# Two thirds of the modulation product moved from TensorE to GpSimd and from the first stages of layer 0 into its attention

## The chip, the cores and the metric

The kernel runs on one core of one Trainium2 chip. The metric is the device time of one execution in microseconds (us). Three runs of the kernel before gave 3046.41, 3048.2 and 3042.95 us: a median of 3046.41 us. TensorE's granted clock has two levels, 1.2 and 2.4 GHz; the profile writes it as a share of the upper one.

## What is computed

A sequence of 1024 tokens with 1024 channels goes through two layers of one block (a gated convolution beside an attention that picks 256 keys for each query), then through one layer of a second block (two recurrences and a feed-forward part). The change touches only how the first block is modulated:

```python
c_act = jax.nn.silu(c)                                   # (1, 1024)
for l in range(2):
    mod = c_act @ w_ada[l] + b_ada[l]                    # (1, 3072)
    shift, scale, gate = jnp.split(mod, 3, axis=-1)
    h = rmsnorm(x, g_pre[l]) * (1.0 + scale[:, None, :]) + shift[:, None, :]
    ...                                                  # h @ w_in, convolution, key search, attention
    x = x + gate[:, None, :] * rmsnorm(y, g_post[l])
```

`c_act @ w_ada[l]` is a product of one row with a 1024 x 3072 matrix in float32. Layer 0 needs its shift and scale before its first projection, its gate only when its output is added to x; layer 1's shift and scale are needed at the end of layer 0, its gate later still.

## The kernel before

**The product in pieces.** `w_ada` comes in 48 pieces of 256 rows by 512 columns (512 KB each, two blocks of 128 rows side by side in SBUF). The list `ADA_PIECES` (line 472) orders them: pieces 0 to 15 are shift and scale of layer 0 (four column blocks n = 0 to 3 of four pieces), 16 to 23 the gate of layer 0 (n = 4, 5), 24 to 31 the gate of layer 1, 32 to 47 shift and scale of layer 1. `ada_piece` (lines 677 to 682) makes two float32 products with 512 columns for each piece. The stationary operand `cb[l]` is `c_act` repeated over 128 columns, so that every partition of the PSUM result holds the same row. Eight products, from four pieces, add up one column block.

**Where the pieces stand on TensorE.** Pieces 0 to 15 run first (line 866). Each other piece is put between other work of layer 0 by `ada_pieces` (line 686): one behind each of the eight groups of transposes of x (`transpose_x`, pieces 16 to 23), eight between the blocks of the index scores (line 934, pieces 24 to 31), and sixteen inside the first two convolution projections (`conv_in` of `wg0` and `wv0`, line 806, pieces 32 to 47).

**What VectorE does with the results.** `gate_sum` (line 1910) adds a gate row of 1024 from PSUM to the bias, `gate_gain` (line 1916) multiplies it by `g_post`. `columns` (line 1889) turns a block of 512 shift or scale values from a row into a column per channel, with a multiplication by the identity and a reduction. `gains` (line 1903) adds the bias and `g_pre`. Those of layer 1 and both gates run beside the search for the key threshold (`beside`, line 2172), which is VectorE's main work after the index scores. `ht_part` (line 1964) scales and shifts the transposed x of layer 0: for each of eight groups one `TENSOR_SCALAR` from PSUM (L1972) and two subtractions (L1980); ScalarE does three operations for the same group (L1330, L1333, L1335).

**Queues.** SyncE issues the weight loads in the order in which they stand in its program (lines 503 to 565). A piece's buffer is one of four (`ADA`, then `ADA2`); piece i waits until piece i - 4 has been multiplied. The other weights come in chunks of 1 MB through two raw buffers (`stage`); GpSimd splits each chunk into a high and a low bf16 part (`CAST` at L646, `TENSOR_TENSOR` at L653; 4 of each for one chunk) into a ring of four. It may overwrite a slot only when TensorE has used the chunk four before it. Pieces 28 to 47 stand in SyncE's program behind chunk `cv1` and ahead of `wv1`.

**Attention of layer 0.** From about 486 to 680 us a loop over 64 steps i = 8 tb + h (query block tb, head h) runs on TensorE, VectorE and ScalarE (lines 1035 to 1053 and 2318 to 2363). In step i TensorE makes the logits of step i, the weighted sums of steps i - 3 and i - 5, and transposes the probabilities of step i - 1. VectorE finds the logits' extreme and writes them to SBUF (L2339), subtracts the high parts (L2319, L2349) and so on. The logits use the PSUM pair `big`, two tiles in turn. In steps 3 to 6 VectorE writes the low part of the convolution's output (L2164), after which the SBUF region from 0 to 4096 is free. GpSimd has only the chunks `oa0` and `oa1` to split there. Each waits for a ring slot: that of `uq`, last used in step 51 of the loop, and that of `uv`, used to its end. Layer 1 runs the same code without any piece.

Of the kernel before, what the change touches and what calls it, by code (L numbers as in the profile page):

```python
# [99 lines left out]
def build(nc, ap, events):  # L100

    ctx = ExitStack()
    with ctx:
# [6 lines left out]
        s_ada_used = ctx.enter_context(nc.semaphore("ada_used"))  # L110
        s_b_gate_in = ctx.enter_context(nc.semaphore("b_gate_in"))
# [80 lines left out]
        readers = (s_act_setup, s_c_out, s_p_out, s_conv_act, s_conv_dve, s_dve_setup, s_dve_step, s_found, s_gemm, s_hf, s_hf_act, s_hgrn_act, s_hgrn_dve, s_ht_lo, s_latent_act, s_latent_dve, s_lmax, s_ot_lo, s_pt_lo, s_qt_lo, s_read_act, s_relu, s_ya_lo, s_yr, s_weigh, s_x_sum, s_x_y, s_ya)  # L192
# [143 lines left out]
        ADA2 = fl(4096, 4096).rearrange("p (r k n) -> p r k n", r=4, k=2)  # L336
# [4 lines left out]
        KID = [bf(at + 4096, 1024), bf(at + 4608, 1024)]  # L341
        at += 5120
# [44 lines left out]
        cb = [PB[1].rearrange("p (k m) -> p k m", k=KT), HFW.rearrange("p (k m) -> p k m", k=KT)]  # L387
        GPR = [RBC, HFW]
# [84 lines left out]
        ADA_PIECES += [(l, n, kp) for l in range(LAYERS) for n in (4, 5) for kp in range(KT // 2)]  # L473
        ADA_PIECES += [(1, n, kp) for n in range(4) for kp in range(KT // 2)]
        ADA_AT = {p: i for i, p in enumerate(ADA_PIECES)}

        def ada_buf(i):
            return (ADA if i < 24 else ADA2)[:, i % 4, :, :]  # L480

# [7 lines left out]
        def _(sp):  # L489
            def ada(i):  # L490
                l, n, kp = ADA_PIECES[i]
                if i >= 4:
                    sp.wait_ge(s_ada_used, when(s_ada_used, i - 4))
                sp.dma_start(ada_buf(i), AP_["w_ada"][l, kp * 2 * P:(kp + 1) * 2 * P, n * 512:(n + 1) * 512].rearrange("(k p) n -> p k n", k=2)) \
                    .then_inc(s_ada_in[i % 4], mark(s_ada_in[i % 4], i, by=16))
# [30 lines left out]
            for i in range(16, 24):  # L526
                ada(i)
            sp.wait_ge(s_rb_out, when(s_rb_out))
            sp.dma_start(TOEP, bass.AP(AP_["rb"].tensor, 0, [[1, P], [384, NH], [1, 2 * P]])).then_inc(s_toep_in, mark(s_toep_in, by=16))
            sp.wait_ge(s_gemm, when(s_gemm, "hx", 0, 1, 3))  # L530
            for i in range(24, 28):
                ada(i)
            for n in range(RAW_RING, len(CHUNKS)):
                weights(n)
                if n == CHUNK_AT[(0, "wg1")]:

                    sp.wait_ge(s_ht_lo, when(s_ht_lo, "all", 0))
                    sp.dma_start(GPR[0], AP_["g_post"][0:1, :].partition_broadcast(P)).then_inc(s_gp_in, mark(s_gp_in, 0, by=16))
# [3 lines left out]
                if n == CHUNK_AT[(0, "cv3")]:  # L542
                    sp.wait_ge(s_ada_used, when(s_ada_used, 47))
                    sp.dma_start(GPR[1], AP_["g_post"][1:2, :].partition_broadcast(P)).then_inc(s_gp_in, mark(s_gp_in, 1, by=16))
                    sp.wait_ge(s_dve_setup, when(s_dve_setup, "gate_row", 0))
                    sp.dma_start(CBROW, AP_["conv_b"][0:1, :].partition_broadcast(P)).then_inc(s_cb_in, mark(s_cb_in, 0, by=16))
                if n == CHUNK_AT[(1, "wg1")]:
                    sp.wait_ge(s_ht_lo, when(s_ht_lo, "all", 1))
                    sp.dma_start(CBROW, AP_["conv_b"][1:2, :].partition_broadcast(P)).then_inc(s_cb_in, mark(s_cb_in, 1, by=16))
# [28 lines left out]
        def _(pool):  # L578
# [79 lines left out]
        def _(pe):  # L658
# [18 lines left out]
            def ada_piece(i, g):  # L677
                l, n, kp = ADA_PIECES[i]
                pe.wait_ge(s_ada_in[i % 4], when(s_ada_in[i % 4], i))
                for k in (2 * kp, 2 * kp + 1):  # L680
                    ins = pe.matmul(g, cb[l][:, k, :], ada_buf(i)[:, k % 2, :], start=k == 0, stop=k == KT - 1)
                ins.then_inc(s_ada_used, mark(s_ada_used, i))

            ada_at = {}

            def ada_pieces(l, n):

                if l:
                    return
                for i in range(n):  # L690
                    m = ada_at.get("next", 16)
                    ada_at["next"] = m + 1
                    if m == 16:
                        ada_at["tile"] = take(pe, "c2", "gate", 0)
                    if m == 24:
                        pe.wait_ge(s_dve_setup, when(s_dve_setup, "cb", 1))
                        ada_at["tile"] = take(pe, "c2", "gate", 1)
                    if m >= 32 and m % 4 == 0:
                        ada_at["tile"] = take(pe, "c", "ada", 1, (m - 32) // 4)
                    half = m // 4 % 2 if m < 32 else 0  # L700
                    ada_piece(m, ada_at["tile"][:, half * 512:(half + 1) * 512])

            def transpose_x(l):

                for half in range(2):
                    for j in range(4):
                        pe.wait_ge(s_xn, when(s_xn, l, half * 4 + j))
                    for kp in range(4):
# [7 lines left out]
                        ada_pieces(l, 1)  # L716
# [89 lines left out]
            def conv_in(l, name, half, ada):  # L806
# [3 lines left out]
                for jh in range(2):  # L810
                    g = take(pe, "big", name, l, half, jh)
                    for jj in range(4):
                        for k in range(KT):
                            ins = mm3(pe, g[:, jj * 256:(jj + 1) * 256], [phase(x[:, k, :], 4 * jh + jj) for x in hT], [x[:, k, :] for x in w], k == 0, k == KT - 1)
                        if jj < 3:
                            ada_pieces(l, ada)
# [3 lines left out]
                    ada_pieces(l, ada)  # L820
# [44 lines left out]
            pe.wait_ge(s_dve_setup, when(s_dve_setup, "cb", 0))  # L865
# [11 lines left out]
            for l in range(LAYERS):  # L877
# [46 lines left out]
                for tb in range(2, NT):  # L924
# [12 lines left out]
                conv_in(l, "wg", 0, 1)  # L937
                conv_in(l, "wv", 0, 1)
                conv_in(l, "wg", 1, 0)
# [3 lines left out]
                conv_in(l, "wv", 1, 0)  # L943
# [92 lines left out]
                for i in range(n + 8):  # L1036
# [231 lines left out]
        def _(act):  # L1268
# [49 lines left out]
            for l in range(LAYERS):  # L1318
# [73 lines left out]
                def conv_x(q):  # L1392
                    act.wait_ge(s_gemm, when(s_gemm, "xt", l, q))
                    if l == 0:
                        act.wait_ge(s_ada_used, when(s_ada_used, 47))
# [8 lines left out]
                def gate_by_token(c, tp):  # L1404
# [5 lines left out]
                    elif l == 0:  # L1410
                        act.wait_ge(s_dve_setup, when(s_dve_setup, "gate_row", 1))
# [460 lines left out]
        def _(dve):  # L1872
# [11 lines left out]
            dve.tensor_copy(cb[0], s_(S_C, 8).unsqueeze(2).broadcast_to((P, 8, P))).then_inc(s_dve_setup, mark(s_dve_setup, "cb", 0))  # L1884
# [3 lines left out]
            def columns(l, n):  # L1888

                dve.wait_ge(s_ada_used, when(s_ada_used, l * 32 + 4 * n + 3))  # L1890
                if l:
                    g, own = tile("c", "ada", 1, n), YC[:, 0, :]
                else:
                    g, own = tile("big", "ada", 0, n // 2)[:, n % 2 * 512:(n % 2 + 1) * 512], RBC[:, 0:512]
# [15 lines left out]
            def gate_sum(l):  # L1910
                dve.wait_ge(s_ada_used, when(s_ada_used, 23 + 8 * l))
                dve.wait_ge(s_b_gate_in, when(s_b_gate_in, LAYERS - 1))
                step(dve.tensor_tensor(gate_row[:, l, :], gate_row[:, l, :], tile("c2", "gate", l)[:, :], ALU.add))  # L1913
                freed_by_step("gate", l)

            def gate_gain(l):
                dve.wait_ge(s_gp_in, when(s_gp_in, l))
                dve.tensor_tensor(gate_row[:, l, :], gate_row[:, l, :], GPR[l], ALU.mult).then_inc(s_dve_setup, mark(s_dve_setup, "gate_row", l))
# [106 lines left out]
            for l in range(LAYERS):  # L2025
# [8 lines left out]
                if l == 0:  # L2034
                    gate_sum(0)
                    dve.wait_ge(s_ht_lo, when(s_ht_lo, "all", 0))
# [824 lines left out]
```

## Time and profile before

| | us |
|---|---|
| median of 3 runs (lowest, highest) | 3046.41 (3042.95, 3048.2) |
| span of the profiled execution, first to last instruction | 3044.6 |
| the profiled execution's own time | not given apart from its span |
| TensorE (PE) busy, 19746 products | 2860.1 (94%) |
| VectorE (DVE) busy | 1953.3 (64%) |
| ScalarE (ACT) busy | 1323.3 (43%) |
| GpSimd (POOL) busy | 1280.0 (42%) |
| mean granted TensorE clock | 0.980 of full speed |
| DMA, mean | 70 GB/s |

The span is the time to compare with; it lies 1.8 us under the median of the runs. Busy time says how long an engine executed instructions, not that they set the end: for that one looks at what each engine waited for in a stretch. Busy times of TensorE are modelled, its start times are not, so the pitch from one start to the next is the safer number.

### The profile page before, as it was taken

The page shows a single profiled execution, that of the slowest core. Times are in us where ns is not written, and L with a number is a line of the kernel's source. Part 1 is how long each engine was busy: PE and PEld are TensorE (multiplying, and loading weights), DVE is VectorE, ACT ScalarE, POOL GpSimd, SP SyncE. Part 2 cuts the span into 40 slices and gives each one's busy share as a digit, 9 for nine tenths or more (in the row PEclk, how much of TensorE's full clock was granted, in tenths as well). Part 3 has the DMA queues.
Part 4 walks back from the last instruction along what each step waited for, and adds up shares of the span by engine and source line. Part 5 has one row for each costly group of instructions (what it writes and reads, how often), then busy time and mean ns, then how long its engine had stood idle before and what let it go on. Part 6 is the DMA issues. An engine that isn't in the chain of part 4 may idle for free.

```text
span 3044.6 us, 49166 instructions
## 1 busy us (share of the span) xinstructions
PE 2860.1 (94%) x19746; PEld 1749.1 (57%) x19746; DVE 1953.3 (64%) x3140; ACT 1323.3 (43%) x2341; POOL 1280.0 (42%) x1060
## 2 busy tenths in 40 slices
PE   7889998999979988999999999999999999999998
PEld 3438776874429667864466565664764444444443
DVE  3785997763589996644875665666663654444445
ACT  3353654652366646643344554454543322122222
POOL 1302482010602580012545846767661635555551
PEclk9999999999989999999999999999999999999999
DMA  8223241002201340021101111201122201111111
GB/s 292 110 70 122 84 154 52 12 22 104 94 14 43 125 139 29 12 87 59 67 29 42 70 42 42 70 31 66 43 85 110 70 28 56 56 56 44 54 44 74
DMA packets 50898, 213.45 MB, mean 70 GB/s; under 512 B 4680, under 2 KB 9968, under 8 KB 34032
## 3 DMA queue, kind: packets, MB, share of 16 engines
q1 hardware_dynamic: 42288, 195.63, 18.5%
q10 hardware_dynamic: 8384, 14.68, 1.4%
q8 instruction: 157, 2.57, 0.3%
q14 instruction: 69, 0.57, 0.1%
HBM read 190.36 MB, written 19.94 MB: 69 GB/s over the span
## 4 chain that ended last, share of the span: by engine, by line
PE 41%; DVE 3%; POOL 3%; ACT 2%; issue 1%; DMA 0%; ACTq 0%; POOLq 0%; DVEq 0%
PE big L284 7%; PE big L286 7%; PE big L285 7%; PE banks L284 4%; PE banks L286 4%; PE banks L285 4%; PE banks L1183 3%; POOL w_lo L596 2%; PE banks L1162 0%; PE banks L1153 0%; PE banks L1134 0%; PE banks L1164 0%; PE banks L1170 0%; DVE arena L2567 0%; DVE arena L2568 0%
## 5 line engine op out<-in xcount | busy, mean ns | idle before, releaser
L653 POOL TENSOR_TENSOR w_lo<-stage,w_hi 128x512 bf16<-128x512 f32 x340 | 429.7, 1295 | 367.3 <-ACT w_hi L1390 367.0
L646 POOL CAST w_hi<-stage 128x512 bf16<-128x512 f32 x252 | 179.6, 753 | 781.4 <-PE big L286 588.5
L284 PE MATMUL big<-w_hi,ht_hi 128*128 128x256 bf16 (+2 forms) x1280 | 358.0, 288 | 22.7 <-DVE arena L1913 4.7
L596 POOL TENSOR_TENSOR w_lo<-stage,w_hi 128x512 bf16<-128x512 f32 x174 | 249.6, 1445 | 263.6 <-ACT w_hi L1590 263.6
L285 PE MATMUL big<-w_lo,ht_hi 128*128 128x256 bf16 (+2 forms) x1280 | 357.9, 288 | 0.0
L286 PE MATMUL big<-w_hi,ht_lo 128*128 128x256 bf16 (+2 forms) x1280 | 357.8, 287 | 0.0
L284 PE MATMUL big<-ht_hi,w_hi 128*128 128x512 bf16 x816 | 310.2, 380 | 24.7 <-POOL w_lo L596 8.7
L286 PE MATMUL big<-ht_hi,w_lo 128*128 128x512 bf16 x816 | 310.0, 380 | 0.0
L285 PE MATMUL big<-ht_lo,w_hi 128*128 128x512 bf16 x816 | 309.8, 380 | 0.0
L284 PE MATMUL big<-arena,w_hi 128*128 128x512 bf16 (+1 forms) x716 | 222.5, 328 | 21.4 <-DVE arena L2154 8.4
L285 PE MATMUL big<-arena,w_hi 128*128 128x512 bf16 (+1 forms) x716 | 222.6, 328 | 0.0
L286 PE MATMUL big<-arena,w_lo 128*128 128x512 bf16 (+1 forms) x716 | 221.9, 327 | 0.0
L2103 DVE TENSOR_SCALAR_CACHE_REDUCE arena<-arena,smalli 128x512 bf16<-128x512 f32 (+5 forms) x268 | 206.7, 827 | 2.4
L1604 ACT ACTIVATE arena<-big 128x512 f32<-128x512 f32 x116 | 68.9, 594 | 315.3 <-PE big L286 315.3
L284 PE MATMUL banks<-w_hi,arena 128*128 128x128 bf16 (+2 forms) x704 | 177.6, 275 | 14.1 <-ACT arena L1840 12.3
L284 PEld LDWEIGHTS big<-w_hi,ht_hi 128*128 128x128 bf16 x1280 | 151.3, 118 | 63.2 <-issue 17.9
L284 PE MATMUL big<-w_hi,arena 128*128 128x512 bf16 (+1 forms) x576 | 179.5, 327 | 4.3 <-DVE arena L2713 2.7
L1466 ACT ACTIVATE arena<-arena,smalli 128x896 bf16<-128x896 f32 x124 | 134.8, 1089 | 105.0 <-DVE smalli L2248 105.0
L285 PE MATMUL big<-w_lo,arena 128*128 128x512 bf16 (+1 forms) x576 | 179.4, 327 | 0.0
L286 PE MATMUL big<-w_hi,arena 128*128 128x512 bf16 (+1 forms) x576 | 179.2, 327 | 0.0
L286 PE MATMUL banks<-w_hi,arena 128*128 128x128 bf16 (+2 forms) x704 | 177.5, 274 | 0.0
L285 PE MATMUL banks<-w_lo,arena 128*128 128x128 bf16 (+2 forms) x704 | 177.5, 274 | 0.0
(395 smaller groups left out, 7144.2 us busy)
## 6 DMA issues: line engine op xcount, KB each, us to landing
stage<-in_w SPq DMA_DIRECT2D x130, 1024.0 KB, 4.8
arena<-in_w_ada SPq DMA_DIRECT2D x48, 512.0 KB, 4.4
arena<-in_x SPq DMA_DIRECT2D x16, 512.0 KB, 9.2
xs<-arena SPq DMA_DIRECT2D x16, 512.0 KB, 2.6
arena<-xs SPq DMA_DIRECT2D x16, 512.0 KB, 7.2
gt<-arena ACTq DMA_DIRECT2D x16, 256.0 KB, 2.5
arena<-gt ACTq DMA_DIRECT2D x16, 256.0 KB, 2.6
out_x<-arena SPq DMA_DIRECT2D x8, 512.0 KB, 2.6
```

The costliest lines, as they stand in the source:

```text
L284: pe.matmul(out, ah, bh, start=start, stop=False, skip_group_check=onto)
L285: pe.matmul(out, ah, bl, start=False, stop=False, skip_group_check=onto)
L286: return pe.matmul(out, al, bh, start=False, stop=stop, skip_group_check=onto)
L596: return pool.tensor_tensor(lo, x, hi, ALU.subtract)
L646: pool.tensor_copy(w_flat[0][:, w0 + c0:w0 + c1], stage[:, n % RAW_RING, c0:c1]).then_inc(s_w_hi_split, mark(s_w_hi_split, n, q))
L653: ins = pool.tensor_tensor(w_flat[1][:, w0 + c0:w0 + c1], stage[:, n % RAW_RING, c0:c1], w_flat[0][:, w0 + c0:w0 + c1], ALU.subtract)
L1183: ins = pe.matmul(g[:, s * 64:(s + 1) * 64].rearrange("p (j h) -> p j h", h=h), KF[c][:, s * P:(s + 1) * P], q, start=True, stop=True)
L1466: ins = act.activation(is_over[tb], score[tb], ACT.Sign, scale=-1.0, bias=smalli[:, 8 + j:9 + j].bitcast(F32), accum_out=s_(S_CNT + j))
L1604: act.activation(quarter(c, out), product(c, b, to), fn).then_inc(s_p_out, mark(s_p_out, c, b, name))
L2103: ins = dve.tensor_scalar(is_over[tb], score[tb], thr(j), 0.0, op, ALU.add, accum_out=cnt[:, j:j + 1])
```

## The change

The 32 pieces 16 to 47 are no longer multiplied on TensorE. Each is loaded during layer 0's attention, and GpSimd multiplies each of its two row blocks by the matching column of `c_act` (one scalar for each partition) and adds them up over the four pieces of a column block. What is left, the sum over the 128 partitions, is one float32 product with a matrix of ones for each of the 8 column blocks (`late_sum`), in the steps 18, 24, 30, 34, 38, 42, 48 and 54 of the attention loop. VectorE's share of each (`gate_sum`, `columns`, `gains`, `gate_gain`) follows in the next step. The pieces use two buffers in the region from 0 to 2048, and the results take a turn of the PSUM pair `big`. The loads of `g_post` move to the same place in SyncE's program; the `conv_b` row is loaded earlier. The second copy of `cb` is gone.

Cut to its core:

```diff
-        ADA_PIECES += [(l, n, kp) for l in range(LAYERS) for n in (4, 5) for kp in range(KT // 2)]
-        ADA_PIECES += [(1, n, kp) for n in range(4) for kp in range(KT // 2)]
+        ADA_LATE = [(0, 4), (0, 5), (1, 4), (1, 5), (1, 0), (1, 1), (1, 2), (1, 3)]
+        ADA_STEP = dict(zip((18, 24, 30, 34, 38, 42, 48, 54), ADA_LATE))
+        ADA_PIECES += [(l, n, kp) for l, n in ADA_LATE for kp in range(KT // 2)]
 
         def ada_buf(i):
-            return (ADA if i < 24 else ADA2)[:, i % 4, :, :]
+            return ADA[:, i % 4, :, :] if i < 16 else ADA2[:, i % 2, :, :]
...
             def ada(i):
-                if i >= 4:
+                if i >= 18:
+                    sp.wait_ge(s_ada_taken, when(s_ada_taken, i - 2))
+                elif 4 <= i < 16:
                     sp.wait_ge(s_ada_used, when(s_ada_used, i - 4))
...
-            for i in range(16, 24):
-                ada(i)
...
-            sp.wait_ge(s_gemm, when(s_gemm, "hx", 0, 1, 3))
-            for i in range(24, 28):
-                ada(i)
             for n in range(RAW_RING, len(CHUNKS)):
                 weights(n)
...
-                if n == CHUNK_AT[(0, "cv1")]:
-                    for i in range(28, 48):
+                if n == CHUNK_AT[(0, "oa1")]:
+                    sp.wait_ge(s_conv_dve, when(s_conv_dve, "yc_lo", 0, 3))
+                    for i in range(16, 48):
                         ada(i)
+                        if i == 17:
+                            sp.dma_start(GPR, AP_["g_post"][0:1, :].partition_broadcast(P)).then_inc(s_gp_in, mark(s_gp_in, 0, by=16))
                     sp.wait_ge(s_dve_setup, when(s_dve_setup, "gate_row", 0))
+                    sp.dma_start(GPR, AP_["g_post"][1:2, :].partition_broadcast(P)).then_inc(s_gp_in, mark(s_gp_in, 1, by=16))
...
+            def late_sums():
+
+                for i in range(16, len(ADA_PIECES)):
+                    l, n, kp = ADA_PIECES[i]
+                    m = ADA_LATE.index((l, n))
+                    x, out = ada_buf(i), ADA_SUM[m % 2]
+                    pool.wait_ge(s_ada_in[i % 4], when(s_ada_in[i % 4], i))
+                    for k in range(2):
+                        pool.tensor_scalar(x[:, k, :], x[:, k, :], s_(S_C + 2 * kp + k), None, ALU.mult).then_inc(s_ada_scaled, mark(s_ada_scaled, i, k))
+                    for k in range(2):
+                        pool.wait_ge(s_ada_scaled, when(s_ada_scaled, i, k))
+                    if kp == 0:
+                        if m >= 2:
+                            pool.wait_ge(s_turn, when(s_turn, "ada", *ADA_LATE[m - 2]))
+                        pool.tensor_tensor(out, x[:, 0, :], x[:, 1, :], ALU.add).then_inc(s_ada_taken, mark(s_ada_taken, i))
+                    else:
+                        pool.wait_ge(s_ada_taken, when(s_ada_taken, i - 1))
+                        pool.tensor_tensor(out, out, x[:, 0, :], ALU.add).then_inc(s_ada_scaled, mark(s_ada_scaled, i, "half"))
+                        pool.wait_ge(s_ada_scaled, when(s_ada_scaled, i, "half"))
+                        pool.tensor_tensor(out, out, x[:, 1, :], ALU.add).then_inc(s_ada_taken, mark(s_ada_taken, i))
+
             for n in range(len(CHUNKS)):
+                if CHUNKS[n] == (0, "oa0"):
+                    late_sums()
...
+            def late_sum(l, n):
+
+                m = ADA_LATE.index((l, n))
+                pe.wait_ge(s_ada_taken, when(s_ada_taken, 16 + 4 * m + 3))
+                g = take(pe, "big", "ada", l, n)[:, 0:512]
+                pe.matmul(g, ones, ADA_SUM[m % 2], start=True, stop=True).then_inc(s_turn, mark(s_turn, "ada", l, n))
...
                         ins.then_inc(s_gemm, mark(s_gemm, "hx", l, half, kp))
-                        ada_pieces(l, 1)
...
-                        if jj < 3:
-                            ada_pieces(l, ada)
...
-                    if tb < NT - 1:
-                        ada_pieces(l, 2 if tb < 5 else 1)
...
                     if 1 <= i <= n:
                         turn(*steps[i - 1])
+                    if l == 0 and i in ADA_STEP:
+                        late_sum(*ADA_STEP[i])
...
+            def late_part(l, n):
+                if n < 4:
+                    columns(l, n)
+                else:
+                    gate_sum(l, n)
+                if (l, n) == (0, 5):
+                    gate_gain(0)
+                if (l, n) == (1, 3):
+                    gains(1)
+                    gate_gain(1)
...
                     if 3 <= i < 7:
                         gated_low(i - 3)
+                    if l == 0 and i - 1 in ADA_STEP:
+                        late_part(*ADA_STEP[i - 1])
```

## Rows read from the trace of the kernel before

**Rows 1.** The page, busy time of each engine in the whole span.

```profile
PE 2860.1 (94%) x19746; PEld 1749.1 (57%) x19746; DVE 1953.3 (64%) x3140; ACT 1323.3 (43%) x2341; POOL 1280.0 (42%) x1060
```

**Rows 2.** Instructions of line 681, the products with pieces (two records for each).

```profile
L681 PE MATMUL banks<-arena x128: 592/592/1193, 51.4 to 284.6; 128*128 128x512 f32 x128
```

**Rows 3.** Timeline of PE, stage of transposes: start, us, engine, line, operation, idle before.

```profile
51.44 3.75 PE L681 MATMUL banks<-arena 128*128 128x512 f32 x4 [7.10 <-DMA arena<-in_w_ada]
...
59.64 1.88 PE L681 MATMUL banks<-arena 128*128 128x512 f32 x4
61.36 1.04 PE L713 MATMUL big<-con,arena 128*128 128x128 f32 x8
...
76.08 0.39 PE L284 MATMUL big<-ht_hi,w_hi 128*128 128x512 bf16 x1 [1.59 <-DVE ht_lo L1980]
```

**Rows 4.** Timelines of DVE and ACT in the same stage.

```profile
46.08 0.81 DVE L1972 TENSOR_SCALAR arena<-big,small 128x512 f32<-128x512 f32 x1
...
62.43 0.81 DVE L1972 TENSOR_SCALAR arena<-big,small 128x512 f32<-128x512 f32 x1 [0.58 <-PE big L713]
63.16 1.28 DVE L1980 TENSOR_TENSOR ht_lo<-arena,ht_hi 128x512 bf16<-128x512 f32 x2
...
63.81 0.61 ACT L1335 ACTIVATE ht_hi<-arena 128x512 bf16<-128x512 f32 x1
```

**Rows 5.** Line 1433, ScalarE's reading of index scores, layer 0 and layer 1.

```profile
L1433 ACT ACTIVATE arena<-big x48: 491/754/1024, 150.9 to 209.4; 128x384 f32<-128x384 f32 x8, 128x512 f32<-128x512 f32 x8, 128x640 f32<-128x640 f32 x8, 128x768 f32<-128x768 f32 x8
...
L1433 ACT ACTIVATE arena<-big x48: 491/759/1037, 860.8 to 909.8; 128x384 f32<-128x384 f32 x8, 128x512 f32<-128x512 f32 x8, 128x640 f32<-128x640 f32 x8, 128x768 f32<-128x768 f32 x8
```

**Rows 6.** Line 829, transposes of the convolution input, layer 0 and layer 1.

```profile
L829 PEld LDWEIGHTS banks<-con,arena x32: 139/141/143, 305.8 to 366.0; 128*128 128x128 f32 x32
...
L829 PEld LDWEIGHTS banks<-con,arena x32: 138/140/143, 972.4 to 1030.2; 128*128 128x128 f32 x32
```

**Rows 7.** Busy time by stretch: PE, PEld, DVE, ACT, POOL, clock, DMA share, GB/s.

```profile
209.40:366.00 156.60, 149.84 (x1139) 120.82 (x1140) 119.48 (x391) 77.22 (x132) 48.62 (x48) 0.97 0.31 100
...
486.60:671.60 185.00, 174.41 (x2134) 150.16 (x2132) 128.78 (x315) 116.56 (x350) 7.70 (x9) 0.97 0.07 23
...
909.80:1030.20 120.40, 118.33 (x1074) 106.37 (x1074) 109.68 (x378) 77.29 (x132) 47.63 (x48) 1.00 0.21 72
```

**Rows 8.** Waits of PE from 212 to 310 us: total, times, longest.

```profile
PE big L284 <- DVE arena L1913: 4.7, 1, 4.7
```

**Rows 9.** Lines 646 and 629: a one-input and a two-input operation of GpSimd, minimum/median/maximum ns.

```profile
L646 POOL CAST w_hi<-stage x252: 602/616/2335, 44.3 to 2975.9; 128x512 bf16<-128x512 f32 x126
...
L629 POOL TENSOR_TENSOR arena<-stage x13: 1257/1263/1268, 2429.8 to 2934.2; 128x512 f32<-128x512 f32 x13
```

**Rows 10.** Timeline of POOL before and in attention of layer 0.

```profile
455.29 6.39 POOL L646 CAST w_hi<-stage 128x512 bf16<-128x512 f32 x4
461.65 7.30 POOL L653 TENSOR_TENSOR w_lo<-stage,w_hi 128x512 bf16<-128x512 f32 x4
...
623.60 2.29 POOL L646 CAST w_hi<-stage 128x512 bf16<-128x512 f32 x4 [136.06 <-PE big L286]
625.85 4.51 POOL L653 TENSOR_TENSOR w_lo<-stage,w_hi 128x512 bf16<-128x512 f32 x4
```

**Rows 11.** DMA issues from 150 to 300 us: count, KB each, median us to landing.

```profile
arena<-in_w_ada SPq DMA_DIRECT2D x20, 512.0 KB, 3.8
```

**Rows 12.** Timeline of DVE, attention of layer 0: L2164's last, L2339 of steps 19, 43, 55.

```profile
498.50 1.22 DVE L2164 TENSOR_TENSOR ht_lo<-arena,ht_hi 128x1024 bf16<-128x1024 f32 x1
...
522.73 0.56 DVE L2339 CUSTOM_DVE_ANT_0 arena<-big,arena 128x384 f32<-128x384 f32 x1 [0.26 <-PE big L999]
...
590.91 0.95 DVE L2339 CUSTOM_DVE_ANT_0 arena<-big,arena 128x768 f32<-128x768 f32 x1
...
638.81 1.08 DVE L2339 CUSTOM_DVE_ANT_0 arena<-big,arena 128x896 f32<-128x896 f32 x1
```

**Rows 13.** Timeline of DVE: the first half of a `columns`.

```profile
43.57 0.69 DVE L1896 TENSOR_TENSOR arena<-big,con 128x512 f32<-128x512 f32 x1 [5.43 <-PE big L681]
```

More of the change, by code:

```diff
@@ L534, in _ @@
                 weights(n)
-                if n == CHUNK_AT[(0, "wg1")]:
-                    sp.wait_ge(s_ht_lo, when(s_ht_lo, "all", 0))
-                    sp.dma_start(GPR[0], AP_["g_post"][0:1, :].partition_broadcast(P)).then_inc(s_gp_in, mark(s_gp_in, 0, by=16))
-                if n == CHUNK_AT[(0, "cv1")]:
-                    for i in range(28, 48):
+                for l in range(LAYERS):
+                    if n == CHUNK_AT[(l, "wg1")]:
+                        sp.wait_ge(s_ht_lo, when(s_ht_lo, "all", l))
+                        sp.dma_start(CBROW, AP_["conv_b"][l:l + 1, :].partition_broadcast(P)).then_inc(s_cb_in, mark(s_cb_in, l, by=16))
@@ L680, in ada_piece @@
                 for k in (2 * kp, 2 * kp + 1):
-                    ins = pe.matmul(g, cb[l][:, k, :], ada_buf(i)[:, k % 2, :], start=k == 0, stop=k == KT - 1)
+                    ins = pe.matmul(g, cb[:, k, :], ada_buf(i)[:, k % 2, :], start=k == 0, stop=k == KT - 1)
                 ins.then_inc(s_ada_used, mark(s_ada_used, i))
[L684 to L701, printed above, removed]
+            def late_sum(l, n):
[3 more added lines that the diff above has]
+                pe.matmul(g, ones, ADA_SUM[m % 2], start=True, stop=True).then_inc(s_turn, mark(s_turn, "ada", l, n))
             def transpose_x(l):
@@ L1888, in columns @@
             def columns(l, n):
-                dve.wait_ge(s_ada_used, when(s_ada_used, l * 32 + 4 * n + 3))
                 if l:
-                    g, own = tile("c", "ada", 1, n), YC[:, 0, :]
+                    dve.wait_ge(s_turn, when(s_turn, "ada", l, n))
+                    g, own = tile("big", "ada", 1, n)[:, 0:512], ADA_OWN
                 else:
+                    dve.wait_ge(s_ada_used, when(s_ada_used, 4 * n + 3))
                     g, own = tile("big", "ada", 0, n // 2)[:, n % 2 * 512:(n % 2 + 1) * 512], RBC[:, 0:512]
@@ L2034, in _ @@
                 if l == 0:
-                    gate_sum(0)
-                    dve.wait_ge(s_ht_lo, when(s_ht_lo, "all", 0))
-                    dve.tensor_copy(cb[1], s_(S_C, 8).unsqueeze(2).broadcast_to((P, 8, P))).then_inc(s_dve_setup, mark(s_dve_setup, "cb", 1))
                     forget_bounds()
@@ L2172, in beside @@
                 def beside(slot):
-                    if l == 0 and slot == 2:
-                        gate_gain(0)
-                    if l == 0 and slot == 5:
-                        columns(1, 0)
-                    if l == 0 and slot == 16:
-                        gate_gain(1)
                     if slot == 6:
@@ L2184, in beside @@
                     if slot == 11:
-                        if l == 0:
-                            for n in range(1, 4):
-                                columns(1, n)
-                            gains(1)
                         conv_pad()
```

54 lines of the change are left out of this document (21 added, 33 removed).

## The prediction

> **What bounds the kernel now.** The page comes first: TensorE is busy for 94% of the span, VectorE for 64% and GpSimd for 42% [rows 1]. So whatever leaves TensorE may pay, but only in stretches where nothing else ends last. The instructions of line 681 show what leaves: 128 records with 512 columns, two for each of 64 products, so 32 pieces, started between 51.4 and 284.6 us [rows 2]. The timeline gives the price: a piece starts at 59.64 and the transposes behind it at 61.36, 1.72 us for a piece and 0.86 for a product [rows 3]. 32 pieces are 55 us of TensorE. Whether they are 55 us of the span is read stretch by stretch, and the best guide is the kernel itself: layer 1 runs the same code without pieces.
>
> **What is removed.**
>
> *Transposes (8 pieces).* TensorE idles 7.10 us for the first late piece, whose load stands far back in SyncE's queue, and then gives 1.72 us to a piece behind each group of transposes [rows 3]. Without pieces the next bound is VectorE's and ScalarE's work on a group. VectorE's starts at 62.43, its subtractions start at 63.16 and take 1.28, together 2.0 us; ScalarE ends the same group at 64.42, 1.99 us after its start [rows 4]. At 2.05 us a group from 46.08 the eighth starts at 60.4, its high parts are there at 62.4, and the subtractions end near 63.8. The first projection, which waits for them, started at 76.08 [rows 3] and would start near 64: a gain of 12. Something is late next: TensorE is then less than half busy, and its clock may stand at 1.2 GHz when the projection starts. After the idle 7.10 us four records took 3.75 us where four take 1.88 [rows 3], a loss of 1.9, which I charge. Net 10; bounds 7 (only the idle time goes) and 13.
>
> *Index scores (8 pieces, 13.8 us).* ScalarE reads the scores from 150.9 to 209.4 us in layer 0 and from 860.8 to 909.8 in layer 1, 58.5 against 49.0 [rows 5]. Here ScalarE and VectorE end last when the pieces are gone, so only part of 13.8 returns: 9.5.
>
> *Projections and search (16 pieces, 27.5 us).* From the last score read to the last transpose of the convolution input layer 0 takes 366.0 - 209.4 = 156.6 us, layer 1 takes 1030.2 - 909.8 = 120.4 [rows 5, 6]: 36.2 less. TensorE's busy time differs by 149.84 - 118.33 = 31.5 and its idle time by the other 4.7 [rows 7]. The idle part is a wait for `gate_sum` at the start of the search [rows 8], which goes too; of the busy part 27.5 are pieces and the rest a lower granted clock, 0.97 against 1.00 [rows 7]. VectorE also loses its gate and column work here. I take 36 and, as the lower bound, the pieces alone, 27.5. A gain above 36 I exclude: layer 1 has TensorE busy for 118.33 of 120.40.
>
> The VectorE copy into `cb` of layer 1 costs nothing today and gives nothing. No other SyncE load is nearer its user than before: with pieces 16 to 47 gone from the front of the queue every chunk of layer 0 is issued as early or earlier.
>
> **What is added, all in layer 0's attention (486.6 to 671.6).** TensorE is busy there for 174.41 of 185.00 us [rows 7], so nearly everything given to it is paid. Eight products with ones at 0.86 are 6.9 us. Each also takes a turn of the `big` pair from the logits, and VectorE must empty it in the next step, ahead of its own part of the probabilities: 0.69 for a gate block, two such operations for a `columns` [rows 13], with completion gaps 0.7 to 1.4 us. Behind that wait on VectorE stand L2319 and L2339, and behind those ScalarE's exponentials and TensorE's next transposes; behind TensorE's own wait stand all logits. The disturbance has no row. From below it is nothing (VectorE is busy 128.78 of 185.00 [rows 7]), from above the whole 1.4. I take 0.6, nearer the lower end because VectorE has 56 us to spare: 1.5 us an event with the product, 12 for eight, and 1 more for the last, which also carries `gains` and `gate_gain`. Sum 13, bounds 7 and 19. A gain from adding work is excluded.
>
> *GpSimd's pace decides whether this holds.* A piece is two scalings and two additions (one for the first of a block). An addition in float32 takes 1.26 us [rows 9]. The scaling has no row: a cast, also one input, takes 0.60 at least and 0.616 in the median, a two-input operation 1.26 [rows 9]. It is nearest to the cast, and I take 0.60. With three completion gaps of 0.1 a piece costs 4.0, a first one 2.7, a block 14.7. The loads have two buffers and land 3.8 us after issue [rows 11], so a pair of pieces cannot take less than 3.8 + 0.2 + 4.0 = 8.0: no slower. I take 15 us a block. In this very stretch four casts took 2.29 and four subtractions 4.51 us [rows 10], the clean pace, though VectorE was at work. The Trainium skill (GPSIMD Engine Reference, section 4.1) calls one-input work on GpSimd roughly line-rate and two-input work about twice as slow as on VectorE; by it the scaling would sit at the cast's end of my bracket, and the sum would be the same.
>
> *When are the sums due?* The region is free at 498.50 + 1.22 = 499.7 [rows 12]. Two loads at once land near 505, so block m (from 0) is ready near 520 + 15 m. It is due just ahead of the logits of the next step, 1 to 2 us before their L2339: 521.8 for step 18, 589.2 for step 42, 637 for step 54 [rows 12], each later by 1.5 for every block already paid. Block 0: 520 against 521.8. Block 5: 595 against 596.7. Block 7: 625 against 647.5. All are in time, two of them barely.
>
> *Queues moved past.* SyncE holds the load of layer 1's first chunk behind the 32 pieces; it could go today only when GpSimd has split `oa0`, after 630.4 [rows 10]. GpSimd holds `oa0` behind the pieces, to about 625 to 650; its user is the output projection behind the loop, which runs to 671.6 and beyond [rows 7]. Both cost nothing while the pace holds.
>
> **The sum.** -10 - 9.5 - 36 + 13 = -42.5, against the profiled span of 3044.6, which lies 1.8 under the median of 3046.41. The rest of the program is untouched. 3046.4 - 42.5 = 3004. A measurement of this kernel tells about 0.2% (6 us) from no change.
>
> **Rivals.**
>
> *Late sums.* If the scaling costs what a two-input operation costs, a piece is 5.3 and a block 20 us. Block 5 is then ready at 505 + 120 = 625 against 596.7, and TensorE stalls about 28 us in all: 3032. For it: float32 output and a scalar for each partition are not in the cast. Against it: the number of inputs.
>
> *Slower: VectorE and GpSimd lock each other out.* Just before attention, beside VectorE work with two inputs in SBUF, four casts took 6.39 us and four subtractions 7.30 [rows 10]. At 1.60 and 1.83 a piece takes 7.2, a first one 5.2, a block 26.8. Block 7 is ready at 505 + 214 = 719 against 647.5: 72 us of stall, 3076. It decides from a block of 23 us on (505 + 8 x 23.3 - 647.5 = 44), 5.8 us a piece. Against it stand the clean 2.29 and 4.51 in the attention itself [rows 10]: most VectorE operands there come from PSUM. The Trainium skill (SBUF, section "Who interferes with whom") has the rule: a VectorE instruction with two SBUF inputs contends with a GpSimd instruction that reads SBUF, and the later one fully blocks. By that rule, the trace agrees on both sides, and the lockout would need another mix than this loop has.
>
> *Less comes back.* Layer 0 is not layer 1: if the transposes give 7, the search stretch only its pieces, 27.5, the sum is -7 - 9.5 - 27.5 + 13 = -31: 3015.
>
> *More comes back.* If VectorE's slack covers the disturbance and the clock holds at the first projection: -12 - 9.5 - 36 + 7 = -50.5: 2996.
>
> **Chances.** Forecast 0.52, late sums 0.17, less 0.15, more 0.10, lockout 0.06. Only the last ends above today's time; a partly late pace could land near it, 0.02 for within 0.2%. The range from 2992 to 3026 takes in the forecast, both size cases and the milder half of late sums.
>
> **What would show it.** Line 681 has 64 records left. The first projection starts near 64 us, not 76. The last transpose of the convolution input comes some 55 us earlier (366.0 now). The attention lasts near 198 instead of 185 us. GpSimd's scalings stand near 0.6 us and its blocks follow each other every 15 us; TensorE has no waits for GpSimd of more than a few us in all. The forecast is wrong if the scaling lies near 1.3, if TensorE waits for the sums in every block, or if the stretch 209.4 to 366.0 shrinks by less than 27.

## The result, and the profile after

The changed kernel takes 3064.96 us in the median of four runs (3059.28 to 3066.39), the kernel before beside it 3046.61. The ratio is 1.0061 with a 95% interval from 1.0047 to 1.0075: slower by 18 us, where 42 us less were forecast. The profiled execution took 3059.28 us with a span of 3057.1, 12.5 more than the span of before; it is the shortest of the four, 5.7 us under their median, so the stages below account for these 12.5 us and not for the whole 18. The sum over stages follows from the same landmarks as in the prediction (in order: first score read, last score read, last transpose of the convolution input, L2339 of steps 0 and 63 of layer 0's attention, which is L2336 now, and the end):

| stretch | before | after | change | forecast |
|---|---|---|---|---|
| start to the first score read | 150.9 | 149.4 | -1.5 | -10 |
| index scores | 58.5 | 49.3 | -9.2 | -9.5 |
| projections and search | 156.6 | 120.4 | -36.2 | -36 |
| rest of the search, choice of keys | 120.6 | 121.8 | +1.2 | 0 |
| attention of layer 0 | 185.0 | 244.0 | +59.0 | +13 |
| everything behind it | 2373.0 | 2372.2 | -0.8 | 0 |

By the start of the attention 45.7 us had been gained, where 55.5 were forecast; most of the shortfall is in the first stretch. The attention then gave the gain back and 13 us more. The first fence holds the landmarks themselves, from the instructions by line (minimum/median/maximum ns, first and last start); the rows of before are [rows 5, 6] and the stretch of [rows 7].

```profile
L1432 ACT ACTIVATE arena<-big x48: 491/759/1045, 149.4 to 198.7; 128x384 f32<-128x384 f32 x8, 128x512 f32<-128x512 f32 x8, 128x640 f32<-128x640 f32 x8, 128x768 f32<-128x768 f32 x8
...
L832 PEld LDWEIGHTS banks<-con,arena x32: 138/140/142, 261.3 to 319.1; 128*128 128x128 f32 x32
...
L2336 DVE CUSTOM_DVE_ANT_0 arena<-big,arena x64: 277/749/1226, 440.9 to 684.9; 128x128 f32<-128x128 f32 x8, 128x256 f32<-128x256 f32 x8, 128x384 f32<-128x384 f32 x8, 128x512 f32<-128x512 f32 x8
```

Two stretches by their busy time, the stage of the transposes and the attention (PE, PEld, DVE, ACT, POOL, clock, DMA share, GB/s), the second to be set beside the 174.41, 0.97 and 7.70 of [rows 7]:

```profile
43.30:72.20 28.90, 11.98 (x67) 9.14 (x65) 27.75 (x29) 16.32 (x25) 27.42 (x25) 0.68 0.52 181
...
440.90:684.90 244.00, 196.53 (x2150) 161.43 (x2148) 145.85 (x331) 116.89 (x350) 181.63 (x129) 0.90 0.30 91
```

TensorE worked for only 22 us more but idled for 47.5 instead of 10.6 us, at a mean clock of 0.90 instead of 0.97. GpSimd went from 7.70 to 181.63 us. What TensorE waited for from 430 to 720 us, from the table of waits (us in total, times, longest):

```profile
PE big L708 <- POOL arena L599: 25.7, 6, 7.0
PE banks L1009 <- DVE arena L2314: 8.1, 14, 1.3
```

Line 708 is the product with ones. It waits for GpSimd's additions 6 times, 25.7 us in all. These six products start at 479.4, 502.0, 525.0, 547.0, 569.7 and 591.7 us, each as soon as its sum is finished, so up to there GpSimd sets the pace of the whole loop. GpSimd's timeline in the middle of this stretch (start, us, line, operation) shows one piece and the start of the next:

```profile
541.08 3.10 POOL L588 TENSOR_SCALAR arena<-arena,small 128x512 f32<-128x512 f32 x2
544.32 1.26 POOL L597 TENSOR_TENSOR arena<-arena 128x512 f32<-128x512 f32 x1
545.66 1.26 POOL L599 TENSOR_TENSOR arena<-arena 128x512 f32<-128x512 f32 x1
546.89 3.11 POOL L588 TENSOR_SCALAR arena<-arena,small 128x512 f32<-128x512 f32 x2
```

And all scalings, from the instructions by line:

```profile
L588 POOL TENSOR_SCALAR arena<-arena,small x64: 1559/1567/2002, 456.9 to 632.5; 128x512 f32<-128x512 f32 x64
```

Two scalings take 3.11 us, two additions and their gaps 2.7, a piece 5.81 in these rows and 5.85 in the median (4.5 for the first of a block, which has one addition); the scaling's minimum is 1.56 us, more than an addition. The first additions of the blocks (L594) start at 460.17, 482.62, 505.12, 528.15, 550.14, 572.90, 594.90 and 617.99: 22.5 us a block, not 15.

The other miss is at the front. VectorE's timeline in the stage of the transposes:

```profile
50.96 2.48 DVE L1992 TENSOR_TENSOR ht_lo<-arena,ht_hi 128x512 bf16<-128x512 f32 x2
...
54.09 1.94 DVE L1992 TENSOR_TENSOR ht_lo<-arena,ht_hi 128x512 bf16<-128x512 f32 x2
...
56.67 3.06 DVE L1992 TENSOR_TENSOR ht_lo<-arena,ht_hi 128x512 bf16<-128x512 f32 x2
```

GpSimd's timeline in the same stage, where it splits the weights of the first chunks:

```profile
47.02 5.88 POOL L672 TENSOR_TENSOR w_lo<-stage,w_hi 128x512 bf16<-128x512 f32 x4
...
56.47 5.85 POOL L672 TENSOR_TENSOR w_lo<-stage,w_hi 128x512 bf16<-128x512 f32 x4
```

And the first products of the first projection in TensorE's timeline:

```profile
72.32 0.61 PE L286 MATMUL big<-ht_hi,w_hi 128*128 128x512 bf16 x1 [9.68 <-DVE ht_lo L1992]
72.72 0.63 PE L287 MATMUL big<-ht_lo,w_hi 128*128 128x512 bf16 x1
73.14 0.63 PE L288 MATMUL big<-ht_hi,w_lo 128*128 128x512 bf16 x1
73.57 0.63 PE L286 MATMUL big<-ht_hi,w_hi 128*128 128x512 bf16 x1
```

A pair of subtractions that took 1.28 us [rows 4] takes 1.94 to 3.06; four subtractions of GpSimd that take 4.51 elsewhere [rows 10] take 5.8. The projection starts at 72.32, not at 64, and its products follow each other at 0.43 us (72.72, 73.14, 73.57) instead of the 0.22 of before: TensorE stands at 1.2 GHz for its first 5 us (granted clock 0.50 from 72.3 to 77.3 us, 1.00 from 77.7 on), after a stage in which it was busy for 11.98 of 28.90 us at a mean clock of 0.68 (the first row by stretches above).

### The profile page after: what moved, and what is told of

It reads as the page before. It is cut to its first block, busy times and chain, and to the rows that moved or that the text cites. A ratio compares the mean times of both kernels' runs of the same rounds, so it can differ in the third digit from the quotient of the medians.

```text
span 3057.1 us, 49089 instructions
## 1 busy us (share of the span) xinstructions
PE 2831.3 (93%) x19634; PEld 1735.1 (57%) x19634; DVE 1959.1 (64%) x3141; ACT 1322.9 (43%) x2341; POOL 1460.6 (48%) x1180
## 4 chain that ended last, share of the span: by engine, by line
PE 41%; DVE 3%; POOL 3%; ACT 2%; issue 1%; ACTq 0%; POOLq 0%; DVEq 0%
PE big L286 7%; PE big L288 7%; PE big L287 7%; PE banks L286 4%; PE banks L288 4%; PE banks L287 4%; PE banks L1186 3%; POOL w_lo L615 2%; PE banks L1156 0%; PE banks L1165 0%; DVE arena L2564 0%; PE banks L1137 0%; DVE arena L2565 0%; PE banks L1167 0%; PE banks L1173 0%
## 5 line engine op out<-in xcount | busy, mean ns | idle before, releaser
L672 POOL TENSOR_TENSOR w_lo<-stage,w_hi 128x512 bf16<-128x512 f32 x340 | 434.8, 1312 | 323.9 <-ACT w_hi L1393 323.9
L615 POOL TENSOR_TENSOR w_lo<-stage,w_hi 128x512 bf16<-128x512 f32 x174 | 249.1, 1442 | 260.9 <-ACT w_hi L1589 260.9
L286 PE MATMUL big<-arena,w_hi 128*128 128x512 bf16 (+1 forms) x716 | 226.1, 331 | 20.8 <-DVE arena L2161 8.3
L287 PE MATMUL big<-arena,w_hi 128*128 128x512 bf16 (+1 forms) x716 | 225.8, 331 | 0.0
L286 PE MATMUL banks<-w_hi,arena 128*128 128x128 bf16 (+2 forms) x704 | 176.2, 273 | 14.1 <-ACT arena L1839 12.4
L657 POOL TENSOR_TENSOR w_lo<-stage,w_hi 128x512 bf16<-128x512 f32 x39 | 56.6, 1480 | 261.1 <-ACT w_hi L1822 261.1
```

The source lines that it names most:

```text
L286: pe.matmul(out, ah, bh, start=start, stop=False, skip_group_check=onto)
L287: pe.matmul(out, ah, bl, start=False, stop=False, skip_group_check=onto)
L615: return pool.tensor_tensor(lo, x, hi, ALU.subtract)
L657: ins = pool.tensor_tensor(lo, x, hi, ALU.subtract)
L672: ins = pool.tensor_tensor(w_flat[1][:, w0 + c0:w0 + c1], stage[:, n % RAW_RING, c0:c1], w_flat[0][:, w0 + c0:w0 + c1], ALU.subtract)
```

## The experiments

Three theories of the attention were put against each other. **A:** GpSimd's pace makes the sums late, and the loss is the lag of the latest sum, that is, how long after its due time the sum is ready that is furthest behind. **B:** the eight products, their turns of the PSUM pair and VectorE's part of them cost it. **C:** GpSimd and VectorE block each other in the attention. For the front, **D:** the two collide there.

### e1: no scaling

```diff
-                    for k in range(2):
-                        pool.tensor_scalar(x[:, k, :], x[:, k, :], s_(S_C + 2 * kp + k), None, ALU.mult).then_inc(s_ada_scaled, mark(s_ada_scaled, i, k))
-                    for k in range(2):
-                        pool.wait_ge(s_ada_scaled, when(s_ada_scaled, i, k))
```

> Leaves out the 64 scalings on GpSimd, so the gates and layer 1's modulation are unscaled sums. Theory A (GpSimd's pace sets the loss): a scaling took 1.56 us and a block 22.3; without them a block takes about 13 us, every sum is in time, TensorE no longer waits for GpSimd, and the attention of layer 0 falls from 244 to near 197 us. Time 3001 + 8 x 1.4 = 3012. Rival B (the added products, their turns of the PSUM pair and VectorE's part cost it): the attention stays above 230 us and the time above 3050. Rival C (GpSimd and VectorE collide on their shared port): the load of additions is the same, so the time falls only by the share of the scalings, to 3040 or more.

Measured: 3020.21 us against 3044.37 of the kernel before, ratio 0.9916 (0.9902 to 0.9931). The attention lasts 202.8 us, TensorE waits for no sum there. Products, turns and VectorE's part were all still in it, so B falls. It came out 8 us above the 3012 of theory A; by e4, 5 of these are missing from what the removal gives, and the eight events (product, turn and VectorE's part) cost 3020.21 - 3005.87 = 14.3 us instead of 11.

### e2: the sums taken later

```diff
-        ADA_STEP = dict(zip((18, 24, 30, 34, 38, 42, 48, 54), ADA_LATE))
+        ADA_STEP = dict(zip((19, 29, 36, 43, 48, 53, 59, 64), ADA_LATE))
```

> Only the steps at which TensorE takes the sums are moved, from 18, 24, 30, 34, 38, 42, 48, 54 to 19, 29, 36, 43, 48, 53, 59, 64, read off the measured pace of 22.3 us a block; GpSimd does the same work. Theory A: the waits of 25.7 us go to a few us, attention near 200 us, time 3015 (3010 to 3020). Rival B: the products and turns are the same, so within 10 us of 3065. Rival C: GpSimd runs beside VectorE as before, so within 10 us of 3065.

Measured: 3019.82 us, ratio 0.9921 (0.9904 to 0.9938). Nothing was taken from GpSimd, TensorE or VectorE; eight numbers were changed. The stretch of the attention by its busy time:

```profile
436.90:637.50 200.60, 182.40 (x2148) 153.10 (x2147) 142.60 (x326) 116.70 (x350) 178.48 (x128) 0.97 0.34 105
```

And TensorE's longest waits from 430 to 720 us:

```profile
PE banks L1009 <- DVE arena L2314: 8.0, 17, 1.0
PE banks L286 <- DVE arena L2346: 5.6, 5, 3.1
PE big L286 <- DVE arena L2307: 5.3, 4, 2.5
```

No wait for GpSimd is left, and TensorE's clock is at 0.97 again, with GpSimd as busy as before (178.48 us). So GpSimd's work beside VectorE is not what cost 45 us, which rules out C for the attention, and the lower clock of the changed kernel was a consequence of its waits. This version, with the change's own work all in it, is faster than both kernels.

### e3: the scaling as a two-input product

```diff
-                        pool.tensor_scalar(x[:, k, :], x[:, k, :], s_(S_C + 2 * kp + k), None, ALU.mult).then_inc(s_ada_scaled, mark(s_ada_scaled, i, k))
+                        pool.tensor_tensor(x[:, k, :], x[:, k, :], s_(S_C + 2 * kp + k).broadcast_to((P, 512)), ALU.mult).then_inc(s_ada_scaled, mark(s_ada_scaled, i, k))
```

> The scaling is written as a two-input product with the column repeated along the row. If it costs what the additions cost, 1.27 us instead of 1.56, a block falls from 22.3 to 20.0 us, the latest sum is late by 34 instead of 48 us, and by theory A the time falls by 14 to 3051 (3046 to 3056). If the repeated operand costs as much as the scalar form, no change from 3065. Rivals B and C expect at most 5 us.

Measured: 3038.49 us, ratio 0.9975 (0.9963 to 0.9987), 26 us below the changed kernel, where 14 were expected, because the operation was cheaper still. All its scalings, from the instructions by line:

```profile
L588 POOL TENSOR_TENSOR arena<-arena,small x64: 1032/1039/1489, 454.6 to 599.4; 128x512 f32<-128x512 f32 x64
```

And the attention by its busy time:

```profile
438.30:658.10 219.80, 189.10 (x2150) 156.44 (x2148) 146.97 (x331) 116.67 (x350) 146.76 (x129) 0.95 0.33 101
```

1.04 us in the median instead of 1.57. A block takes 18 to 19 us (L594 at 456.82, 475.05, 493.98, 513.11 and on), and the attention 219.8 us. That is a second point on theory A's line. Against the same kernel's free attention in e2 (200.6) the changed kernel loses 43.4 us and this one 19.2. The lag can be read for block 5: its sum is finished at 591.7 us in the changed kernel and at 566.3 here. It is due 1.5 us before the L2339 of step 43, which is at 590.91 before [rows 12]; shifted to the start of each attention (486.6 before, 440.9 and 438.3 now) that is 543.7 and 541.1. So the lag is 48 and 25 us, without what the events themselves add: 23 us less lag, 24 us less time.

### e4: nothing late

```diff
-                    for i in range(16, 48):
-                        ada(i)
+                    for i in range(17, 18):
                         if i == 17:
...
-                if CHUNKS[n] == (0, "oa0"):
-                    late_sums()
...
-                    if l == 0 and i in ADA_STEP:
-                        late_sum(*ADA_STEP[i])
...
-                if n < 4:
-                    columns(l, n)
-                else:
-                    gate_sum(l, n)
```

> Leaves out the 32 late pieces altogether: their loads, scalings, additions, the eight products and VectorE's reading of them (gates and layer 1's modulation are then wrong); gains and gate_gain stay. What is left is what the removal gives by itself. Theory A: the early gain of 46 to 47 us is whole, the attention is back at 186 us, time 3001 (2998 to 3004); e1 less this run is the price of eight products with their turns, 8 x 1.4 = 11 us. If the attention stays longer than 190 us or the rest of the program changes, the early gain is not what the first trace shows.

Measured: 3005.87 us, ratio 0.9865 (0.9849 to 0.9881). The stretch of the attention:

```profile
440.20:627.10 186.90, 175.06 (x2136) 150.48 (x2133) 131.18 (x319) 116.46 (x350) 7.71 (x9) 0.97 0.09 28
```

The attention lasts 186.9 us, against 185.0 before and 184.7 in layer 1 of the same trace. The removal alone is worth 38.5 us: 5 less than expected, of the size of this run's own spread (2999.31 to 3007.91). Its trace shows 46.4 us gained by the start of the attention, 1.9 lost in it and 5.9 behind it (2378.9 instead of 2373.0), where nothing was edited. Over all ten traces that last stretch takes between 2372.0 and 2385.2 us, so a difference of a few us between two traces says little by itself. e2 less e4 is 13.9 us for eight events, 1.7 each. The two attentions differ by 13.7, though e2 has only seven events in this stretch: its last product is at 642.4 us, behind the 637.5 where the stretch ends. The forecast had 13 for the eight.

### e5: GpSimd waits with the second chunk

On top of e2:

```diff
                 if CHUNKS[n] == (0, "oa0"):
                     late_sums()
+                if CHUNKS[n] == (0, "kvk"):
+                    pool.wait_ge(s_ht_lo, when(s_ht_lo, "all", 0))
```

> On top of e2: GpSimd splits the second weight chunk only when the transposed x of layer 0 is split (one wait more on GpSimd). Theory D (in the stage of transposes GpSimd's splits and VectorE's subtractions, both with two SBUF inputs, slow each other: 1.1 to 1.5 us for a subtraction instead of 0.68, 5.9 us for four splits instead of 4.5): the first projection starts at 66 us instead of 72.3 and the time falls by 4 to 6, to about 3015. Rival: the subtractions are slow for another reason (their place behind ScalarE), the start stays near 72 and the time within 2 us of e2 (3019.8).

Measured: 3014.17 us (3008.13 to 3015.71) against 3043.43 of the kernel before, ratio 0.9896 (0.9883 to 0.991), 5.6 below e2. It was measured in another round than e2; e6 below, of the same round and without this edit, took 3021.28, 7.1 more, and the two intervals do not meet. VectorE's timeline in the stage of the transposes:

```profile
46.10 2.80 DVE L1994 TENSOR_TENSOR ht_lo<-arena,ht_hi 128x512 bf16<-128x512 f32 x2
...
53.63 1.28 DVE L1994 TENSOR_TENSOR ht_lo<-arena,ht_hi 128x512 bf16<-128x512 f32 x2
...
55.55 1.28 DVE L1994 TENSOR_TENSOR ht_lo<-arena,ht_hi 128x512 bf16<-128x512 f32 x2
```

And GpSimd's:

```profile
42.26 2.28 POOL L667 CAST w_hi<-stage 128x512 bf16<-128x512 f32 x4 [40.70 <-DMA stage<-in_w]
44.51 5.41 POOL L674 TENSOR_TENSOR w_lo<-stage,w_hi 128x512 bf16<-128x512 f32 x4
61.95 4.43 POOL L667 CAST w_hi<-stage 128x512 bf16<-128x512 f32 x4 [12.03 <-DVE ht_lo L1994]
```

Where GpSimd is silent, from 50 to 62 us, every pair of subtractions takes 1.28 us and the groups follow each other at 1.92 us. The first pair still overlaps the first chunk's split and takes 2.80. Theory D holds. GpSimd resumes at 61.95, when the last subtraction ends, the first product recorded of the projection stands at 62.34 (expected: 66), and the first score is read at 139.1 us, against 149.4 in the changed kernel and 147.2 in e2. Not all of it is this edit's: the whole front of this execution ran earlier, as its first split at 42.26 us shows (44.78 in the changed kernel, 43.06 in e2). That leaves 7.3 us against e2. The attention is shorter too, 195.8 us against 200.6 in e2 and 199.8 in e6; why is not shown.

### e6: later steps with the cheaper scaling

The edits of e2 and e3 together.

> e2's steps with e3's cheaper scaling (1.05 us instead of 1.56), so a block takes about 18 us instead of 22. Theory A: with e2's steps every sum is in time already, so a faster GpSimd gives nothing: 3020, within 3 us. If GpSimd's load itself costs (a shared port, rival C), 28 us less work on it gives 5 us or more.

Measured: 3021.28 us (3014.83 to 3024.08), ratio 0.9926 (0.9912 to 0.9939), against 3019.82 for e2; its attention takes 199.8 us. Some 30 us less work on GpSimd gave nothing, though the same edit had given 26 us with the steps of the change. GpSimd's time counts only through the lag.

### e7: four events of two blocks

On top of e5 and with e3's scaling; `late_sum` and `late_part` take two blocks each:

```diff
-        ADA_STEP = dict(zip((18, 24, 30, 34, 38, 42, 48, 54), ADA_LATE))
+        ADA_STEP = dict(zip((26, 38, 48, 57), zip(ADA_LATE[0::2], ADA_LATE[1::2])))
...
+                for half, (l, n) in enumerate((first, second)):
+                    m = ADA_LATE.index((l, n))
+                    pe.wait_ge(s_ada_taken, when(s_ada_taken, 16 + 4 * m + 3))
+                    if g is None:
+                        g = take(pe, "big", "ada", l, n)
+                    slot[("ada", l, n)] = slot[("ada", *first)]
+                    pe.matmul(g[:, half * 512:(half + 1) * 512], ones, ADA_SUM[m % 2], start=True, stop=True).then_inc(s_turn, mark(s_turn, "ada", l, n))
```

> Two column blocks share one turn of the PSUM pair, so four events instead of eight, at steps 26, 38, 48 and 57; with the cheaper scaling of e3 and the wait of e5. e2 less e4 puts an event at 13.9 / 8 = 1.7 us, of which the product is 0.86. If the turn and VectorE's interruption make up the rest, four events less give 4 x 0.8 = 3 us below e5: 3012. If it is the products and VectorE's operations themselves, nothing below e5. If the sums come late again (GpSimd holds only two), TensorE waits for GpSimd and the time rises.

Measured: 3019.8 us (3012.66 to 3021.26), ratio 0.9911 (0.9897 to 0.9924): not below e5 but 5.6 above it, with an attention of 206.6 against 195.8 us. TensorE did not wait for GpSimd. It waited longer for VectorE: from 430 to 640 us 9.3 us for L2322 where e5 has 6.5 for the same operation, 4.8 for L2368 where e5 has 1.7, and 3.1 for L1920, the reading of a gate pair, where e5 lists none. Half the turns with twice the work in each gained nothing, so the turn by itself is not shown to be what an event costs beyond its product. That one long interruption of VectorE costs more than two short ones would fit these waits, but no run separates it from the other steps of this kernel.

### e8: filler products

On top of e5:

```diff
                         ins.then_inc(s_gemm, mark(s_gemm, "hx", l, half, kp))
+                        for k in range(2):
+                            pe.matmul(bank[3], cb[:, k, :], ada_buf(12)[:, k, :], start=True, stop=True)
```

> On top of e5: two float32 products with 512 columns into an unused PSUM bank behind each group of transposes of layer 0, as busy work of the size of the old pieces. If the slow clock at the first projection (pitch 0.43 instead of 0.22 us for its first 5 us in the changed kernel) comes from TensorE's idleness ahead of it, the projection starts at the full clock and the time falls by 2 to 3 us below e5. If the clock there has another cause, no change, or up to 2 us more where the filler delays the transposes.

Measured: 3014.46 us (3007.28 to 3015.63), ratio 0.9896 (0.9882 to 0.9909): the same as e5. Early products of the first projection from TensorE's timeline, the first and the last of five starts in a row, in e5:

```profile
62.77 0.63 PE L288 MATMUL big<-ht_hi,w_lo 128*128 128x512 bf16 x1
...
64.47 0.63 PE L286 MATMUL big<-ht_hi,w_hi 128*128 128x512 bf16 x1
```

And in this run:

```profile
66.36 0.38 PE L288 MATMUL big<-ht_hi,w_lo 128*128 128x512 bf16 x1
...
67.22 0.38 PE L286 MATMUL big<-ht_hi,w_hi 128*128 128x512 bf16 x1
```

In e5 the four steps from one row to the other take 1.70 us, 0.43 each; here 0.86, 0.22 each. So the slow clock came from TensorE's idleness ahead of it: with work there (TensorE busy for 19.28 of the 20.86 us before 65.9) the projection runs at 2.4 GHz from the start: the granted clock is 1.00 from 66 to 71 us, and 0.50 from 62.3 to 67.0 in e5. Little of that is left in the time. Counted from the first split (45.04 us here, 42.26 in e5) the rows shown stand at 21.3 us here and 20.5 in e5, so the filler made the start of the projection some 0.8 us later, and the first score, at 140.7 us against 139.1, is read 1.2 us earlier. The two times cannot resolve that.

## Why the prediction was wrong

**The step that failed** is this one: "The scaling has no row: a cast, also one input, takes 0.60 at least and 0.616 in the median, a two-input operation 1.26. It is nearest to the cast, and I take 0.60." It takes 1.56 us, above both ends. A piece was to cost 4.0 us and costs 5.85, a block 15 and takes 22.5. This step alone takes the whole gain: by the prediction's own working, with a block of 22.5 us block 5 is ready at 505 + 135 = 640 against 596.7, a stall of 43 us, and 3004 + 43 = 3047, no change. That the kernel became slower needs the second miss, the transposes below, as well.

**The bracket was wrong, not only the choice in it.** Its upper end was the two-input operation, as if one tensor input could not cost more than two. e3 shows the contrary on the same data: 1.04 us as a two-input product. The rule from the Trainium skill that was set beside it (GPSIMD Engine Reference, section 4.1, one-input work roughly line-rate) agrees with the cast's row and not with this operation; the measurement decides. The rival of late sums had the right mechanism and put 20 us on a block; it had a chance of 0.17, and the lockout rival, which alone went above today's time, was named for the wrong cause. Its threshold, a block of 23.3 us, lies just above the measured 22.5. The 5.8 us a piece beside it does not follow from that block: with a cheaper first piece, as in the prediction's own count, a block of 23.3 needs more than 6 us a piece.

**The transposes** were to give 10 us and gave 1.5. The pace of a group, 2.05 us, was read from rows in which GpSimd was silent. Without the pieces the groups move ahead into the time in which GpSimd splits the first chunks, and both sides slow down (e5). The rule that the prediction quoted against the attention (the Trainium skill, SBUF — State Buffer, section "Who interferes with whom": a VectorE instruction with two SBUF inputs contends with a GpSimd instruction that reads SBUF) fits here, where both operands of the subtractions lie in SBUF: 1.94 to 3.06 us for a pair instead of 1.28. Whether the later of two instructions is blocked fully, as the prediction had it, these merged rows do not show. The clock's loss had been charged at 1.9 us and was 2.5: 12 products at 0.43 instead of 0.22.

**What was right.** The index scores gave 9.2 (forecast 9.5) and the projections with the search 36.2 (36): layer 1 was a good model of layer 0 without its pieces. Products, turns and VectorE's part cost 13.9 us (13), by e2 less e4. The schedule argument held in its form, due times against ready times; e2 turned it into a version that is 25 us faster than the kernel before by changing nothing but the due times. Behind the attention the changed kernel's trace differs from that of before by 0.8 us.

**The sum again, with measured terms:** -1.5 - 9.2 - 36.2 + 1.2 + 59.0 - 0.8 = +12.5, the difference of the two spans. Of the 59.0, 13.7 are the events, 43.4 the lag and 1.9 what the attention of e4 takes more than that of before. Against the forecast of -42.5 the 55 us are 43.4 of lag, 8.5 at the transposes and 3.1 in all other rows together. As TensorE lived it, the 43.4 against e2 are 196.53 - 182.40 = 14.1 us more busy time for the same products, at a granted clock of 0.90 instead of 0.97, and 29.3 us more idle time, of which 25.7 are the waits for GpSimd.

**What stays open:** why the scalar form of the scaling takes 1.56 us; and what makes up the 0.8 us that an event costs beside its product. Open is also why the part behind the attention varies by up to 13 us between traces; that part holds the 5 us by which e4 came out above what was expected.

## What to carry to other kernels

Work moved to an idle engine is paid in the lag of its latest result behind the step that takes it: write ready times beside due times, and put the taking steps after the measured pace before judging the move. Price an operation that the trace does not show by measuring it alone; neither its number of inputs nor the time of a similar operation bounds it. And ask what an engine freed from a wait will now run beside: the stage that was to speed up moved into another engine's way.

## What the runs showed of the hardware

- GpSimd multiplies 128 x 512 float32 values by one scalar for each partition in 1.56 us in the scalar form, but in 1.04 us as a two-input product with the column repeated along the row; an addition of two full tiles takes 1.27 us, a cast to bf16 0.60.
- Beside GpSimd's weight splits a VectorE subtraction of 128 x 512 values from two SBUF operands rose from 0.64 to between 0.97 and 1.5 us in the means of its pairs, and four GpSimd subtractions from 4.51 to 5.8 us. In the attention, where most of VectorE's operations read one operand from PSUM, GpSimd kept its pace (1.57 and 1.27 in the median) for 180 us.
- With TensorE busy for 11.98 of 28.9 us ahead of the first projection, its products started 0.43 us apart at a granted clock of 0.50; with filler work there (busy for 19.28 of 20.86 us), 0.22 apart at 1.00.
